# GpSimd multiplies the probabilities of every second attention unit, in place of VectorE

## The chip, the cores and the metric

The kernel runs on one core of one Trainium2 chip. The metric is the device time of one execution in microseconds. The kernel before takes 1446.1 us (median of three runs, 1443.93 to 1446.41). The engines of a core work side by side and are tied together by semaphores only: TensorE (PE in the profile, with PEld for its weight loads), VectorE (DVE), ScalarE (ACT), GpSimd (POOL) and the queue of SyncE (SP).

## The reference, cut to what matters

The program is one inference step of a one-layer decoder: a projection, three kinds of attention or recurrence side by side (forgetting attention, native sparse attention, HGRN2), an output projection, and a mixture of experts. The change lies in the attention over the 1024 prompt tokens. For every head and block of 128 queries four score matrices are formed, softmaxed over the keys and multiplied with values:

```python
def fox_attend(q, qc, qpos, k, v, kc, kpos):          # "fox": all keys up to the query
    s = jnp.einsum('bqhd,bkhd->bhqk', q, k) * scale
    s = s + qc[..., None] - kc[:, :, None, :]           # decay; masked above the diagonal
    p = jax.nn.softmax(s, axis=-1)
    return jnp.einsum('bhqk,bkhd->bqhd', p, v)
# "cmp": masked softmax over up to 63 compressed keys, with a position bias
# "slc": the same over the selected blocks (with 16 blocks and 16 chosen: all keys up to the query)
# "win": the same over the last 512 keys
def masked_softmax(s, valid):
    s = jnp.where(valid, s, NEG)
    m = jnp.max(s, axis=-1, keepdims=True)
    e = jnp.where(valid, jnp.exp(s - m), 0.0)
    return e / jnp.maximum(jnp.sum(e, axis=-1, keepdims=True), TINY)
```

The three sparse results are weighted by gates and added up.

## The kernel before, in words

The prompt attention is the stage `attn` of each engine's program. It runs over 64 units, `PAIRS`: four heads, in each eight blocks of 128 queries (i = 0 to 7), for each block an even unit with the kinds fox and slc and an odd unit with win and cmp. Within a head I number the units u = 0 to 15, so that u = 2i is the even and u = 2i + 1 the odd unit of block i. In an even unit both kinds have 128 (i + 1) keys. In an odd unit win has 128 (i + 1) keys up to 640, and cmp 7, 15, 23 and so on up to 63.

A unit goes through the engines like this (the lines are those of the profile):

- TensorE writes scores into PSUM banks called `vec` (L851). There are four of them, used in turn.
- VectorE reads a bank, adds the bias from SBUF, writes the scores to SBUF and keeps the running minimum; that is one custom instruction with a small read of the accumulator behind it (L1787).
- ScalarE takes the exponentials and their sum (L1360).
- VectorE's `normalise` makes two factors per query from the sums: a `scalar_tensor_tensor` over 2 columns (L1797, event `exps` waited for), a reciprocal over 2 columns (L1799), and then two multiplications of the unit's scores by the factors, in place (L1803, event `probs`).
- TensorE transposes the probabilities, 128 columns at a time, into PSUM banks called `turned` (L863), ScalarE copies them to SBUF (L1353), and TensorE multiplies them with the values (L875, L876 for even units, L882, L884 for odd ones).

Each engine's program is written out in order, and the order is shifted between them. TensorE does scores(d), transposes(d - 2), values(d - 3). VectorE does scores(d), normalise(d - 1). So the probabilities of unit d - 2 are due when TensorE is through with the scores of unit d.

GpSimd has one kind of work in this stage, the table `foxdiag`: the decays of a head with the mask of the diagonal added, 128x1024 (L2167 for head 0, L2170 for the others). The table for head h + 1 needs the decays `cumf` of that head, which VectorE makes behind the scores of u = 8 of head h (`decay_rows`, L1763, eight small instructions), ahead of normalise(7). It is first read at u = 0 of head h + 1.

Of the kernel before, what the change touches and what calls it, by code (L numbers as in the profile page):

```python
# [9 lines left out]
ALU = mybir.AluOpType  # L10
# [3 lines left out]
P = 128  # L14
# [204 lines left out]
def program(nc, ctx, I, O_, known):  # L219
# [26 lines left out]
    def skew(base, offset, *dims):  # L246

        return bass.AP(base.tensor, base.offset + offset, [list(base.ap[0])] + [list(d) for d in dims])
# [55 lines left out]
    small = z.take(4 * 16, 4)  # L304
# [81 lines left out]
    def unit_keys(kind, i):  # L386

        if kind == "cmp":
            return 0, min(8 * i + 7, NCMP), 1
        first = max(0, i - 4) if kind == "win" else 0  # L390
        return first * P, (i + 1 - first) * P, i + 1 - first
# [21 lines left out]
    def score_tiles(d):  # L413

        return Sw[d // 2 % 2] if d % 2 else S[d // 2 % 2]
# [205 lines left out]
    def _(e):  # L621
# [231 lines left out]
        def transposes(d):  # L853
            h, i, kinds = PAIRS[d]
            e.wait_ge(*E.at(("probs", d)))
            for j, kind in enumerate(kinds):
                _, L, nb = unit_keys(kind, i)
                for a in range(0, nb, 4):
                    e.wait_ge(*E.free("turned"))
                    bk = E.bank("turned")  # L860
                    for c in range(min(4, nb - a)):
                        n = min(P, L)
                        last = e.transpose(bk[:n, c * P:(c + 1) * P], score_tiles(d)[j][:, (a + c) * P:(a + c) * P + n], ident)  # L863
                    last.then_inc(*E.filled("turned", ("probs turned", d)))
# [333 lines left out]
    def _(e):  # L1198
# [135 lines left out]
        for it in range(n + 4):  # L1334
            d = it - 4
            if d >= 0 and d % 2:
                h, i, _ = PAIRS[d]
                e.wait_ge(*E.full("summed"))
                bk = E.job("summed")
                e.copy(QT[:, h, i * P:(i + 1) * P], bk[:, 0:P]).then_inc(*E.drained("summed", "prompt attention done"))  # L1340
            d = it - 2
            if 0 <= d < n:
                h, i, kinds = PAIRS[d]
                for j, kind in enumerate(kinds):
                    _, L, nb = unit_keys(kind, i)
                    w = min(P, L)
                    for a in range(0, nb, 4):
                        k = min(4, nb - a)
                        e.wait_ge(*E.full("turned"))
                        bk = E.job("turned")  # L1350
                        if d >= 2:
                            e.wait_ge(*E.at(("values", d - 2)))
                        e.copy(turned_tiles(d)[j][:w, a:a + k, :], bk[:w, 0:k * P].rearrange("p (c n) -> p c n", c=k)).then_inc(*E.drained("turned", ("pt", d, j)))  # L1353
            if it < n:
                h, i, kinds = PAIRS[it]
                for j, kind in enumerate(kinds):
                    _, L, _ = unit_keys(kind, i)
                    e.wait_ge(*E.at(("scores", it, j)))
                    s, sm_ = score_tiles(it)[j][:, 0:L], small[:, it % 4]
                    act(s, s, ACT.Exp, scale=-1.0, bias=sm_[:, least(i, kind, j):least(i, kind, j) + 1], accum_out=sm_[:, j:j + 1]).then_inc(*E.done(("exps", it)))  # L1360
# [127 lines left out]
    def _(e):  # L1488
        E = Engine(ev, e, "vector")
        E.banks = banks  # L1490
        tt, ts, stt, cp = e.tensor_tensor, e.tensor_scalar, e.scalar_tensor_tensor, e.tensor_copy
# [61 lines left out]
        for h in range(H):  # L1553
# [68 lines left out]
            for g in range(2):  # L1622
                e.wait_ge(*E.full("vec"))
                bk = E.job("vec")
                for c in range(4):
                    n = 4 * g + c
                    e.wait_ge(*E.own())
                    i = stt(Sall[:, n + 1, :], Sall[:, n, :], ebl[:, n:n + 1], bk[:, c * P:(c + 1) * P], ALU.mult, ALU.add)
                    i.then_inc(*(E.done() if c < 3 else E.drained("vec", ("states", h))))
            e.wait_ge(*E.at(("s0", h)))  # L1630
            for g in range(2):
# [4 lines left out]
                for c in range(4):  # L1636
                    b = 4 * g + c
                    i = stt(VM[:, b, :], S0[:, b, :], ebl[:, 8 + b:9 + b], bk[:, c * P:(c + 1) * P], ALU.mult, ALU.add)
# [17 lines left out]
        for t in range(NT):  # L1656
# [3 lines left out]
            if t == 8:  # L1660
                for g in range(4):
                    s, o = slice(NS * g, NS * g + NS), slice(g * P, (g + 1) * P)
# [12 lines left out]
        for t in range(NT):  # L1675
# [3 lines left out]
            if t == 8:  # L1679
                for g in range(4):  # L1680
                    s, o = slice(NS * g, NS * g + NS), slice(g * 100, g * 100 + 100)
# [110 lines left out]
        def normalise(d):  # L1792

            h, i, kinds = PAIRS[d]
            sm_ = small[:, d % 4]
            e.wait_ge(*E.at(("exps", d)))
            stt(sm_[:, 2:4], sm_[:, 0:2], TINY, skew(GI, 16 * i + 4 * h + 2 * (d % 2), [1, 2]), ALU.max, ALU.mult).then_inc(*E.done())  # L1797
            e.wait_ge(*E.own())
            e.reciprocal(sm_[:, 2:4], sm_[:, 2:4]).then_inc(*E.done(("factors", d)))  # L1799
            e.wait_ge(*E.own())  # L1800
            for j, kind in enumerate(kinds):
                s = score_tiles(d)[j][:, 0:unit_keys(kind, i)[1]]
                ts(s, s, sm_[:, 2 + j:3 + j], None, ALU.mult).then_inc(*E.done(("probs", d)))  # L1803

        n = len(PAIRS)
        decay_rows(0)
        for it in range(n + 1):
            if it < n:
                scores(it)
                if it % 16 == 8 and it + 16 < n:  # L1810
                    decay_rows(it // 16 + 1)
            if it >= 1:
                normalise(it - 1)
# [310 lines left out]
    def _(e):  # L2124
        E = Engine(ev, e, "gpsimd")
# [37 lines left out]
        for d, (h, i, kinds) in enumerate(PAIRS):  # L2163
            if d % 16 == 0:
                if h == 0:
                    e.wait_ge(*E.at(("cumf", h)))
                    tt(foxdiag[h % 2], cumf[h % 2].rearrange("p (t k) -> p t k", t=8), C["diagmask"].unsqueeze(1).to_broadcast([P, 8, P]), ALU.add).then_inc(*E.done(("foxdiag", h)))  # L2167
            if d % 16 == 9 and h + 1 < H:
                e.wait_ge(*E.at(("cumf", h + 1)))
                tt(foxdiag[(h + 1) % 2], cumf[(h + 1) % 2].rearrange("p (t k) -> p t k", t=8), C["diagmask"].unsqueeze(1).to_broadcast([P, 8, P]), ALU.add).then_inc(*E.done(("foxdiag", h + 1)))  # L2170
        E.stage("p5")
        e.wait_ge(*E.at("prompt attention done"))
        e.wait_ge(*E.at("kv_out"))
# [67 lines left out]
```

## Time and profile before

| quantity | value |
|---|---|
| median of the runs | 1446.1 us |
| the profiled execution's own time | 1446.41 us |
| its span, first to last instruction | 1444.5 us |
| prompt attention in it | about 630 to 868 us |
| PE busy over the span | 1255.2 us, 87% |
| DVE busy | 723.4 us, 50% |
| ACT busy | 419.2 us, 29% |
| POOL busy | 165.4 us, 11% |
| mean granted TensorE clock | 0.933 |

The profiled execution's time is 1.9 us more than its span, and 0.3 us more than the median. The shares are means over very different stages, so that what an edit is worth must be read in the stage that it touches. A busy TensorE in this profile is one whose matmuls follow each other without a hole; the holes are what the stage can win back on the other engines.

### The profile page before, as it was taken

What the parts mean: (1) busy time and instruction counts of PE and PEld (TensorE: products, weight loads), DVE (VectorE), ACT (ScalarE), POOL (GpSimd) and SP (SyncE); (2) the same over time, 40 slices, a digit from 0 to 9 for tenths busy, and PEclk for the clock granted to TensorE, in tenths of its full rate; (3) what the DMA queues carried; (4) which work ended last, traced back from release to release, by engine and by line L of the source; (5) the groups of instructions that cost most, each with busy time, mean ns of one, the idle gap of its engine ahead of it and who ended that gap; (6) DMA issues with size and microseconds to landing.
All of it is one profiled execution on the core that took longest, in us unless ns stands there. A gap on an engine that the chain in (4) does not pass through costs nothing.

```text
span 1444.5 us, 19401 instructions
## 1 busy us (share of the span) xinstructions
PE 1255.2 (87%) x6870; PEld 760.5 (53%) x6870; DVE 723.4 (50%) x1614; ACT 419.2 (29%) x882; POOL 165.4 (11%) x191
## 2 busy tenths in 40 slices
PE   3699999999999999979999999999549999999600
PEld 1468787787877555546676675444223333333200
DVE  5526574675744111257768663345643333333288
ACT  2232231422422010135666762212201111111133
POOL 0003021031211000200000000000011111111130
PEclk9799999999999999959999999999759999999955
DMA  9802020130201204306000006300396967668471
GB/s 307 248 24 59 17 74 1 31 59 17 70 5 46 96 6 83 99 12 168 25 25 1 2 1 190 121 29 30 134 314 219 341 196 269 215 221 282 144 272 69
DMA packets 123237, 163.17 MB, mean 113 GB/s; under 512 B 29763, under 2 KB 98547, under 8 KB 123160
## 3 DMA queue, kind: packets, MB, share of 16 engines
q1 hardware_dynamic: 108840, 112.75, 25.7%
q0 software_dynamic: 14320, 49.41, 9.8%
q8 instruction: 47, 0.77, 0.2%
q14 instruction: 30, 0.25, 0.1%
HBM read 225.01 MB, written 36.45 MB: 181 GB/s over the span
## 4 chain that ended last, share of the span: by engine, by line
PE 78%; DVE 14%; ACT 3%; DMA 2%; issue 2%; SPq 0%; POOL 0%; DVEq 0%; ACTq 0%; POOLq 0%
PE act L650 15%; PE vec L1157 11%; PE vec L917 9%; PE vec L679 7%; PE vec L851 5%; PE vec L700 4%; PE act L863 4%; PE act L875 2%; PE act L1170 2%; PE vec L1170 2%; PE act L882 2%; DVE arena L2116 2%; PE vec L815 1%; DMA arena<-x_rows,arena 1%; PE vec L660 1%
## 5 line engine op out<-in xcount | busy, mean ns | idle before, releaser
L650 PE MATMUL act<-arena 128*128 128x352 f32 x768 | 239.1, 467 | 0.4 <-issue 0.4
L650 PEld LDWEIGHTS act<-arena 128*128 128x128 f32 x768 | 145.5, 193 | 76.9 <-issue 3.4
L1157 PE MATMUL vec<-arena 128*64 128x512 f32 x768 | 172.5, 601 | 2.9 <-issue 2.9
L917 PE MATMUL vec<-arena 128*128 128x512 f32 (+1 forms) x288 | 126.3, 593 | 0.4 <-ACT arena L1340 0.4
L1787 DVE CUSTOM_DVE_ANT_0 arena<-vec,arena 128x128 f32<-128x128 f32 (+9 forms) x200 | 86.8, 459 | 60.3 <-PE vec L851 50.3
L1157 PEld LDWEIGHTS vec<-arena 128*64 128x64 f32 x768 | 54.1, 138 | 104.4 <-issue 104.1
L679 PE MATMUL vec<-arena 128*128 128x512 f32 (+1 forms) x256 | 99.9, 546 | 0.0
L2079 DVE TENSOR_SCALAR arena<-arena 128x256 f32<-128x256 f32 x24 | 7.1, 296 | 172.1 <-ACT arena L1451 172.1
L1353 ACT COPY arena<-act 128x512 f32<-128x512 f32 (+11 forms) x176 | 63.7, 431 | 81.7 <-PE act L863 81.6
L851 PE MATMUL vec<-arena 64*128 64x512 f32 (+11 forms) x352 | 84.2, 475 | 3.2 <-DVE arena L1787 2.0
L917 PEld LDWEIGHTS vec<-arena 128*128 128x128 f32 (+1 forms) x288 | 50.8, 180 | 67.5 <-issue 66.2
L1360 ACT ACTIVATE arena<-arena 128x640 f32<-128x640 f32 (+15 forms) x128 | 81.6, 643 | 16.5 <-DVE arena L1787 16.4
L863 PE MATMUL act<-arena 128*128 128x128 f32 (+4 forms) x440 | 66.3, 288 | 6.8 <-DVE arena L1803 6.1
L679 PEld LDWEIGHTS vec<-arena 128*128 128x128 f32 x256 | 47.8, 190 | 44.9 <-issue 27.7
L1613 DVE COPY_PREDICATED arena<-arena,vec 128x512 f32<-128x512 int32 x64 | 44.5, 729 | 48.3 <-PE vec L700 46.5
L700 PEld LDWEIGHTS vec<-arena 128*128 128x128 f32 x512 | 61.9, 192 | 9.3 <-DVE arena L1596 3.2
L660 PE MATMUL vec<-arena 128*128 128x128 f32 (+1 forms) x576 | 65.3, 275 | 0.0
L660 PEld LDWEIGHTS vec<-arena 128*128 128x128 f32 (+1 forms) x576 | 64.5, 183 | 1.3
L700 PE MATMUL vec<-arena 128*128 128x128 f32 x512 | 62.7, 276 | 2.4 <-DVE arena L1596 2.4
L863 PEld LDWEIGHTS act<-arena 128*128 128x128 f32 (+4 forms) x440 | 47.3, 143 | 28.0 <-DVE arena L1803 11.5
L851 PEld LDWEIGHTS vec<-arena 64*128 64x128 f32 x352 | 42.3, 195 | 34.2 <-issue 14.9
L1451 ACT ACTIVATE arena<-vec 128x256 f32<-128x256 f32 x24 | 9.2, 385 | 165.7 <-PE vec L1157 165.7
(371 smaller groups left out, 1832.8 us busy)
## 6 DMA issues: line engine op xcount, KB each, us to landing
arena<-in_exp_w SPq DMA_DIRECT2D x144, 1024.0 KB
y_rows<-arena POOLq DMA_DIRECT2D x48, 256.0 KB, 5.1
arena<-in_w_in SPq DMA_DIRECT2D x16, 512.0 KB, 6.8
arena<-in_x_prompt SPq DMA_DIRECT2D x8, 512.0 KB, 10.0
x_spill<-arena POOLq DMA_DIRECT2D x8, 512.0 KB, 5.6
arena<-x_spill SPq DMA_DIRECT2D x8, 512.0 KB, 4.9
arena<-in_cache_fox_kv SPq DMA_DIRECT2D x16, 256.0 KB, 3.5
x_rows<-arena POOLq DMA_DIRECT2D x8, 512.0 KB, 2.9
```

What stands on the lines that cost most here:

```text
L650: last = mm(bk[:, 0:n], W[k % 2][:, c, m * P:(m + 1) * P], xT[:, c, a:a + n], start=c == 0, stop=c == NC - 1)
L660: last = mm(bk[:r, o:o + P], xT[:, c, t * P:t * P + r], W[h % 2][:, c, 3 * P:4 * P], start=c == 0, stop=c == NC - 1)
L679: last = mm(bk[:r, 0:width], xT[:, c, t * P:t * P + r], w[:, c, 0:width], start=c == 0, stop=c == NC - 1)
L700: last = mm(bk[:, c * P:(c + 1) * P], a[:, ch], b[:, ch], start=True, stop=True)
L851: mm(bk[:, 0:n], QT[s, h, i * P:(i + 1) * P], k[:, first + a:first + a + n], start=True, stop=True).then_inc(*E.filled("vec"))
L863: last = e.transpose(bk[:n, c * P:(c + 1) * P], score_tiles(d)[j][:, (a + c) * P:(a + c) * P + n], ident)
L917: last = mm(bk[:r], src, Wo[:, c, half * 512:(half + 1) * 512], start=c == 0, stop=c == NC - 1)
L1157: last = mm(gu_bank[p][o], xgT[p][:, c, o], Wgu[:, slot, c, :], start=c == 0, stop=c == NC - 1)
L1170: last = mm(dn_bank[half][o], hT[p][:, f, o], Wd[:, slot, f, half * 512:(half + 1) * 512], start=f == 0, stop=f == 1)
L1353: e.copy(turned_tiles(d)[j][:w, a:a + k, :], bk[:w, 0:k * P].rearrange("p (c n) -> p c n", c=k)).then_inc(*E.drained("turned", ("pt", d, j)))
L1360: act(s, s, ACT.Exp, scale=-1.0, bias=sm_[:, least(i, kind, j):least(i, kind, j) + 1], accum_out=sm_[:, j:j + 1]).then_inc(*E.done(("exps" ...
L1787: ins = e.tensor_tensor_reduce(out=s[:, a + o:a + o + w], in0=bk[:, o:o + w], in1=bias, scale=1.0, scalar=prior, op0=ALU.add, op1=ALU.min, ...
```

## The change

VectorE keeps the first two steps of `normalise` (L1797, L1799) for all units, and the two multiplications of the even units. The two multiplications of an odd unit are issued by GpSimd, which first waits for the event `factors` of that unit (the reciprocal). TensorE's wait for `probs` of an odd unit is thereby a wait for GpSimd's counter. In GpSimd's order they stand behind the `foxdiag` of the same iteration.

```diff
             e.reciprocal(sm_[:, 2:4], sm_[:, 2:4]).then_inc(*E.done(("factors", d)))
-            e.wait_ge(*E.own())
-            for j, kind in enumerate(kinds):
-                s = score_tiles(d)[j][:, 0:unit_keys(kind, i)[1]]
-                ts(s, s, sm_[:, 2 + j:3 + j], None, ALU.mult).then_inc(*E.done(("probs", d)))
+            if d % 2 == 0:
+                e.wait_ge(*E.own())
+                L = (i + 1) * P
+                for j in range(2):
+                    s = score_tiles(d)[j][:, 0:L]
+                    ts(s, s, sm_[:, 2 + j:3 + j], None, ALU.mult).then_inc(*E.done(("probs", d)))
...
         # in GpSimd's loop over the units, behind foxdiag:
+            if d % 2:
+                e.wait_ge(*E.at(("factors", d)))
+                for j, kind in enumerate(kinds):
+                    s = score_tiles(d)[j][:, 0:unit_keys(kind, i)[1]]
+                    e.tensor_scalar(s, s, small[:, d % 4, 2 + j:3 + j], None, ALU.mult).then_inc(*E.done(("probs", d)))
```

64 of VectorE's 128 multiplications move. The orders of TensorE and ScalarE stay as they are. VectorE's order at the decays of the next head, which lie between the scores of u = 8 and normalise(7); L1763 is the last step of the decays, ISA 128x512 the custom instruction on the scores of u = 9. Before:

```order
L1763 TENSOR_SCALAR arena<-vec,arena 128x128 x7
L1797 SCALAR_TENSOR_TENSOR arena<-arena 128x2
L1799 RECIPROCAL arena<-arena 128x2
L1803 TENSOR_SCALAR arena<-arena 128x512
L1803 TENSOR_SCALAR arena<-arena 128x31
L1787 ISA arena<-vec,arena 128x512
L1787 ISA arena 128x1
L1787 ISA arena<-vec,arena 128x39
L1787 ISA arena 128x1
L1787 ISA arena<-vec,arena 128x128
L1787 ISA arena 128x1
L1797 SCALAR_TENSOR_TENSOR arena<-arena 128x2
```

VectorE's order at the same place after the change (L1805 is what L1803 was, for u = 8 here):

```order
L1763 TENSOR_SCALAR arena<-vec,arena 128x128 x7
L1797 SCALAR_TENSOR_TENSOR arena<-arena 128x2
L1799 RECIPROCAL arena<-arena 128x2
L1787 ISA arena<-vec,arena 128x512
L1787 ISA arena 128x1
L1787 ISA arena<-vec,arena 128x39
L1787 ISA arena 128x1
L1787 ISA arena<-vec,arena 128x128
L1787 ISA arena 128x1
L1797 SCALAR_TENSOR_TENSOR arena<-arena 128x2
L1799 RECIPROCAL arena<-arena 128x2
L1805 TENSOR_SCALAR arena<-arena 128x640 x2
```

The 512 and the 31 columns of u = 7 have left VectorE's queue, and the scores of u = 9 stand right behind the reciprocal. GpSimd's order before, for the whole attention (L2176 belongs to the stage behind it):

```order
L2167 TENSOR_TENSOR arena<-arena 128x1024
L2170 TENSOR_TENSOR arena<-arena 128x1024 x3
L2176 MEMSET arena 128x512
L2176 MEMSET arena 128x256 x2
L2176 MEMSET arena 128x128
```

GpSimd's order after the change, from u = 5 to u = 9 of a head (L2172 is the `foxdiag` of the next head, L2177 the multiplications):

```order
L2177 TENSOR_SCALAR arena<-arena 128x384
L2177 TENSOR_SCALAR arena<-arena 128x23
L2177 TENSOR_SCALAR arena<-arena 128x512
L2177 TENSOR_SCALAR arena<-arena 128x31
L2172 TENSOR_TENSOR arena<-arena 128x1024
L2177 TENSOR_SCALAR arena<-arena 128x640
L2177 TENSOR_SCALAR arena<-arena 128x39
```

The `foxdiag` of the next head, which had an empty queue ahead of it, now stands behind the multiplications of u = 7, which wait for the reciprocal that VectorE issues behind the decays.

## Rows read from the trace of the kernel before

**Rows 1.** Busy us by engine in two stretches: stretch, length, engines, PEclk, DMA, GB/s
```profile
728.00:752.00 24.00, 23.98 (x200) 17.52 (x199) 16.60 (x63) 17.04 (x48) 0.00 (x0) 1.00 0.11 37
716.00:720.00 4.00, 2.24 (x12) 1.39 (x11) 3.86 (x11) 1.38 (x5) 2.00 (x1) 1.00 0.00 0
```
**Rows 2.** Waits from 630 to 862 us: engine, line, waited for, total us, times, longest
```profile
DVE arena L1787 <- PE vec L851: 50.3, 55, 2.4
PE act L863 <- DVE arena L1803: 6.1, 5, 1.8
```
**Rows 3.** GpSimd's tables: one in the timeline, and the group of three
```profile
716.86 2.00 POOL L2170 TENSOR_TENSOR arena<-arena 128x1024 f32<-128x1024 f32 x1 [57.89 <-DVE arena L1797]
...
L2170 POOL TENSOR_TENSOR arena<-arena 128x1024 f32<-128x1024 f32 x3 | 6.0, 1999 | 141.0 <-DVE arena L1797 141.0
```
**Rows 4.** VectorE's timeline in head 1, at the next decays: start us, us, instruction
```profile
716.69 0.15 DVE L1797 SCALAR_TENSOR_TENSOR arena<-arena 128x2 f32<-128x2 f32 x1
716.88 0.17 DVE L1799 RECIPROCAL arena<-arena 128x2 f32<-128x2 f32 x1
717.08 2.21 DVE L1803 TENSOR_SCALAR arena<-arena 128x512 f32<-128x512 f32 x2
...
720.45 0.15 DVE L1797 SCALAR_TENSOR_TENSOR arena<-arena 128x2 f32<-128x2 f32 x1
...
720.84 1.02 DVE L1803 TENSOR_SCALAR arena<-arena 128x640 f32<-128x640 f32 x2
```
**Rows 5.** TensorE's timeline at the same place
```profile
716.02 1.57 PE L851 MATMUL vec<-arena 64*128 64x512 f32 x6
719.35 0.77 PE L863 MATMUL act<-arena 128*128 128x128 f32 x5 [1.76 <-DVE arena L1803]
...
722.57 1.66 PE L863 MATMUL act<-arena 128*128 128x128 f32 x10
```
**Rows 6.** GpSimd: a line's min/median/max ns; groups with busy us, mean ns, idle before
```profile
L2142 POOL TENSOR_TENSOR arena<-arena x28: 1097/1292/1555, 113.8 to 422.3; 128x512 f32<-128x512 f32 x20, 128x528 f32<-128x528 f32 x8
...
L2134 POOL TENSOR_TENSOR arena<-arena 128x1056 f32<-128x1056 f32 x4 | 11.2, 2795 | 125.6 <-DVE arena L1576 125.6
...
L2176 POOL MEMSET arena<- 128x256 f32 x2 | 0.6, 312 | 0.0
...
L2176 POOL MEMSET arena<- 128x512 f32 x1 | 0.5, 525 | 90.8 <-ACT arena L1340 90.8
```
**Rows 7.** Timelines of both engines at the odd units 3, 5 and 9 of head 1
```profile
702.92 0.50 DVE L1803 TENSOR_SCALAR arena<-arena 128x256 f32<-128x256 f32 x2
...
707.73 0.57 DVE L1803 TENSOR_SCALAR arena<-arena 128x384 f32<-128x384 f32 x2
...
725.56 0.71 DVE L1803 TENSOR_SCALAR arena<-arena 128x640 f32<-128x640 f32 x2
...
703.48 0.55 PE L863 MATMUL act<-arena 128*128 128x128 f32 x3
...
708.55 0.66 PE L863 MATMUL act<-arena 128*128 128x128 f32 x4
...
727.04 0.33 PE L863 MATMUL act<-arena 128*128 128x128 f32 x1
```
**Rows 8.** Both engines in an earlier stage; of two lines min/median/max ns
```profile
108.24 2.79 POOL L2134 TENSOR_TENSOR arena<-arena 128x1056 f32<-128x1056 f32 x1 [52.20 <-DVE arena L1576]
...
L1592 DVE TENSOR_TENSOR arena<-arena x28: 684/704/2925, 108.7 to 420.4; 128x512 f32<-128x512 f32 x20, 128x528 f32<-128x528 f32 x8
...
L1602 DVE TENSOR_TENSOR arena<-vec,arena x8: 675/677/691, 116.4 to 392.1; 128x512 f32<-128x512 f32 x8
```
**Rows 9.** Head 0: TensorE at the same place, and a stretch with the clock
```profile
659.46 0.86 PE L863 MATMUL act<-arena 128*128 128x128 f32 x5 [1.76 <-DVE arena L1803]
...
668.72 0.55 PE L863 MATMUL act<-arena 128*128 128x128 f32 x3
...
662.00:663.00 1.00, 1.00 (x6) 0.51 (x4) 0.00 (x0) 0.02 (x1) 0.00 (x0) 0.50 0.09 17
```

## The prediction

> **What bounds the kernel now.** I first read the busy times by stretch. In the wide units of the attention TensorE is busy 23.98 of 24 us at the full granted clock, VectorE 16.60 [rows 1]. Then the waits: VectorE waits for TensorE's scores 50.3 us in 55 places, TensorE for VectorE's multiplications 6.1 us in five, the longest 1.8 [rows 2]. So VectorE isn't the bound, and work taken from it is worth nothing by itself. Time lies only in TensorE's holes. One is plain: from 716 to 720 us TensorE is busy for 2.24 of 4 us [rows 1], and the timelines say why. VectorE's multiplications of unit 7 start at 717.08 and last 2.21 us; TensorE's transposes of that unit stand at 719.35 behind a hole of 1.76 [rows 4, 5]. A `foxdiag` runs on GpSimd from 716.86 to 718.86 [rows 3], and it holds the multiplication up: the pair of 384 and 23 columns takes 0.57 us, that of 640 and 39 takes 0.71 [rows 7], so this one of 512 and 31 should take some 0.64. The group of such tables has three members [rows 3], one in each of heads 0 to 2, and the hole in head 0 is also 1.76 [rows 9].
>
> **What the change removes there.** VectorE issues no multiplication of unit 7. GpSimd does it first and the table behind it. I work out head 1, by the profiled times.
>
> What one pair costs on GpSimd no row shows. The nearest are: a memset, which only writes, at 312 ns for 256 and 525 ns for 512 columns [rows 6], hence 0.83 ns a column and 0.1 us fixed, the low end; a two-input operation, 2.00 us for 1024 columns [rows 3] and at least 1.10 for 512 [rows 6], hence 1.76 ns a column and 0.2 fixed; and 2.79 us for 1056 columns under load [rows 6, 8], 2.65 a column, the high end. A multiplication by a factor reads one array and writes one; I take 1.0 ns a column and 0.15 us fixed, nearest to the memset. GpSimd's start behind VectorE's result I take at 0.08 us, a little over the 0.06 that TensorE needs (719.35 against an end at 719.29 [rows 4, 5]).
>
> - The reciprocal ends at 717.05 [rows 4]. GpSimd starts at 717.13 and needs 0.66 + 0.18 = 0.84, so 717.97. The transposes start 0.06 us behind at 718.03 instead of 719.35: 1.32 us gained.
> - What is late next: the table now runs from 717.97 to 719.97. VectorE meanwhile does the scores of unit 9 and comes to the factors of unit 8, two SBUF inputs, and to its multiplications, both of the kinds that have been seen waiting for GpSimd [rows 4, 8]. From that factor step to the multiplications are 0.39 us, and these take 1.02 [rows 4], so they end at 719.97 + 1.41 = 721.38, and the transposes of unit 8 start at 721.44. TensorE's own work would bring it there at 718.03 + 3.22 = 721.25 [rows 5]. Against 722.57 the gain is 1.13.
> - Head 2 is like head 1; in head 0 the transposes of unit 8 come later (half clock, below), so its 1.32 stays.
>
> That makes 1.32 + 2 x 1.13 = 3.58 us.
>
> In head 0 the granted clock is 0.5 (1.2 GHz) in the stretch behind the hole [rows 9], and from the transposes of unit 7 to those of unit 9 it takes 668.72 - 659.46 = 9.26 us, in head 1 727.04 - 719.35 = 7.69 at full clock [rows 5, 7, 9]. Those 1.57 us lie behind a hole of 1.76, which would shrink to 0.4; but the same hole in head 1 cost no clock [rows 1]. I count half, 0.8 us.
>
> **What it adds.** TensorE waits for GpSimd in every odd unit. VectorE's pair started 0.03 us behind the reciprocal and took 0.50 us (unit 3), 0.57 (unit 5) and 0.71 (unit 9); TensorE took up the result 0.06, 0.25 and 0.77 us behind its end [rows 7], so that 0, 0.19 and 0.71 us are free.
>
> - Unit 3, 256 + 15 columns: 0.08 + 0.41 + 0.17 = 0.65 against 0.53, late by 0.12, nothing free. Three heads (head 0 has half clock and room there): 0.36 us.
> - Unit 5, 384 + 23: 0.08 + 0.53 + 0.17 = 0.79 against 0.60, 0.19 late and 0.19 free: 0.
> - Unit 9, 640 + 39: 0.08 + 0.79 + 0.19 = 1.06 against 0.74, 0.32 late, 0.71 free: 0. Later units have the same 640 columns and more of TensorE's work ahead, and unit 1 is the narrowest; I count none of them.
>
> Behind the waiting GpSimd instruction only the next odd unit and the tables are queued, and a table isn't read until the next head. VectorE's freed time lies in its waits for scores [rows 2]: 0. The even multiplications meet GpSimd only beside the tables: a side unit's GpSimd pair is through in about 1 us, while VectorE first has two or three score instructions of the next unit.
>
> Sum: -3.58 - 0.8 + 0.36 = -4.0 us on 1446.41, that is 1442.4; the median lies 0.3 below the profiled time, and I say 1442.3.
>
> **What the skill says.** The rows show a VectorE operation with two SBUF inputs at 2.9 instead of 0.68 us beside a GpSimd operation, and one with a PSUM and an SBUF input at 675 to 691 ns whatever ran beside it [rows 8]. The Trainium skill (SBUF — State Buffer, "Who interferes with whom") has this as a lock on a shared port pair, taken for a whole instruction by GpSimd and by VectorE's two-port modes or two-input operations; the trace agrees. By that rule the score instructions stay free, as in my sum. The skill's Perfetto Trace Analysis ("Optimizing Scalar/DVE Operations") warns that moving work between these two engines might not help for that reason; taken literally it would make the gain zero. GPSIMD Engine Reference ("4.1 Engine selection") calls one-input operations about line rate there; an estimate of 0.83 ns a column at its 1.2 GHz would take 0.5 us off my loss and add as much gain.
>
> **The rivals.**
>
> *GpSimd multiplies at the two-input rate* (1.76 ns a column, 0.2 fixed). Unit 3: 0.08 + 0.65 + 0.23 = 0.96 against 0.53, 0.43 late, three times 1.3. Unit 5: 1.20 against 0.60, less the free 0.19, three times 0.41: 1.2. Unit 7 of head 3 about 0.4, unit 9 1.68 against 0.74 less 0.71, with head 3 some 1.2 together. Loss 4.1. At the tables GpSimd ends at 718.49, the gain is 0.8 at unit 7, and the table then ends at 720.49 and unit 8's pair at 721.90: 0.6. Gain 2.0 and no clock won. 1448. For it: the only elementwise operations in the trace run so. Against: they read two arrays.
>
> *The custom score instruction is held too.* Its inputs are like those of the free one in [rows 8], but it never ran beside GpSimd in the trace. Then VectorE stands through unit 7's pair and the table until 719.97, has 2.65 us to the end of unit 8's pair (719.21 to 721.86 now), so 722.62: nothing gained in heads 1 and 2. -1.3 + 0.4 = -0.9: 1445.3.
>
> *Slower: GpSimd is slow enough to be the bound of odd units.* Place: TensorE's transposes of units 3 to 13. At 2.65 ns a column unit 9 takes 2.31 us against 0.74, 0.86 beyond what is free, unit 3 0.67, unit 5 0.77; over 18 such units with 0.5 to 0.9 each about 13 us, less 0.6 at the tables: 1459. Interpolated between this and the two-input rate, it is slower than before by 0.2% from about 1.85 ns a column. Against: those 2.79 us include a wait, since VectorE's operation of 0.68 us had started before and the next took until GpSimd was through [rows 8].
>
> **How the numbers follow.** The forecast has 0.63, the two-input rate 0.14, the held score instruction 0.11, the slow GpSimd 0.12. About 0.2% (2.9 us) is what a measurement can tell from no change. The forecast's own range is 1440.5 (the whole clock term, the memset's rate) to 1444.5 (no clock, losses doubled); three quarters of it lie below 1443.2, which gives faster 0.47. The two-input rate and the held instruction count as same, with the rest of the forecast: 0.39, and the slower one, with a little of the two-input case, 0.14. The range for 8 in 10 is 1440 to 1448.5.
>
> **What the profile would show.** GpSimd's pair of 640 and 39 columns in about 1 us; the hole ahead of unit 7's transposes 0.4 instead of 1.76 us, in three heads; the table right behind unit 7's pair, and unit 8's factor step or multiplication lengthened beside it; score instructions as long as before, also beside GpSimd's work; no new waits of TensorE for GpSimd above 0.2 us. I am wrong if GpSimd's 640 columns take over 1.2 us, or if TensorE's holes at unit 8 take back what unit 7 gives.

## The result and the profile after

| | before | after |
|---|---|---|
| median, us (four runs each, on one chip) | 1445.01 | 1465.81 |
| lowest to highest | 1443.4 to 1446.41 | 1460.02 to 1466.76 |
| profiled execution's own time / its span | 1446.41 / 1444.5 | 1462.62 / 1460.7 |

The ratio is 1.0128, 95% interval 1.01 to 1.0155; it takes in three more runs of the kernel after (1462.62, 1462.97 and 1459.45), so it is a little below the quotient of the two medians. The change makes the kernel 1.3% slower. I had forecast 4 us less; it is about 20 us more. The page of the kernel after, its busy line and the shares of the chain that ended last:

```profile
PE 1260.3 (86%) x6870; PEld 762.0 (52%) x6870; DVE 704.1 (48%) x1550; ACT 419.4 (29%) x882; POOL 225.9 (15%) x255
...
PE 72%; DVE 17%; POOL 4%; ACT 3%; DMA 2%; issue 2%; SPq 0%; DVEq 0%; ACTq 0%; POOLq 0%
```

GpSimd has 60.5 us more to do, VectorE 19.3 less: each microsecond taken from VectorE costs three on GpSimd. And GpSimd, which was 0% of that chain before, is now 4% of it. The groups of GpSimd's multiplications, shapes apart (busy us, mean ns of one, idle before them and what ended it); the neighbours from which I guessed them are in [rows 3, 6]:

```profile
L2177 POOL TENSOR_SCALAR arena<-arena 128x640 f32<-128x640 f32 x16 | 30.2, 1886 | 95.8 <-DVE arena L1799 95.8
L2172 POOL TENSOR_TENSOR arena<-arena 128x1024 f32<-128x1024 f32 x3 | 6.9, 2310 | 0.0
...
L2177 POOL TENSOR_SCALAR arena<-arena 128x256 f32<-128x256 f32 x4 | 3.7, 927 | 15.8 <-DVE arena L1799 15.8
```

640 columns take 1886 ns, 256 take 927: 2.50 ns a column, and 0.29 us fixed. That is 2.5 times the rate I took, and nearly the far end of my range (2.65). VectorE needed 0.71 us for a pair of 640 and 39 columns [rows 7]; GpSimd needs 1.89 + 0.40. The waits in the attention, which answer to [rows 2]:

```profile
DVE arena L1787 <- PE vec L851: 88.3, 61, 3.2
...
PE act L863 <- POOL arena L2177: 18.8, 25, 1.6
```

TensorE's wait for multiplications grew from 6.1 us in five places to 18.8 in 25, none of them long. VectorE's freed time became waiting for scores, 50.3 before and 88.3 now, in a stage that is also 18 us longer. Now head 1 in GpSimd's timeline, at units 3, 5, 7 and 9, and the decays' table behind unit 7:

```profile
696.78 1.25 POOL L2177 TENSOR_SCALAR arena<-arena 128x256 f32<-128x256 f32 x2 [3.67 <-DVE arena L1799]
...
703.54 1.58 POOL L2177 TENSOR_SCALAR arena<-arena 128x384 f32<-128x384 f32 x2 [5.51 <-DVE arena L1799]
...
713.76 1.92 POOL L2177 TENSOR_SCALAR arena<-arena 128x512 f32<-128x512 f32 x2 [8.64 <-DVE arena L1799]
715.64 2.33 POOL L2172 TENSOR_TENSOR arena<-arena 128x1024 f32<-128x1024 f32 x1
...
723.55 2.26 POOL L2177 TENSOR_SCALAR arena<-arena 128x640 f32<-128x640 f32 x2 [5.58 <-DVE arena L1799]
```

and TensorE's transposes of the same units 3, 5, 7, 8 and 9; before, the holes ahead of them were 0 at units 3, 5 and 9 [rows 7] and 1.76 at unit 7 [rows 5]:

```profile
698.08 0.55 PE L863 MATMUL act<-arena 128*128 128x128 f32 x3 [0.85 <-POOL arena L2177]
...
705.18 0.44 PE L863 MATMUL act<-arena 128*128 128x128 f32 x2 [0.37 <-POOL arena L2177]
...
715.74 1.17 PE L863 MATMUL act<-arena 128*128 128x128 f32 x5 [1.53 <-POOL arena L2177]
...
720.53 1.66 PE L863 MATMUL act<-arena 128*128 128x128 f32 x10
725.87 1.28 PE L863 MATMUL act<-arena 128*128 128x128 f32 x6 [0.80 <-POOL arena L2177]
```

The hole at unit 7, on which the whole gain rested, went from 1.76 to 1.53. The slow multiplication took the place of the held one. Every odd unit from 3 to 13, but for unit 7, has a new hole, in all four heads (unit 7 of head 3, which had none, has one of 0.94). VectorE's timeline around 715 us shows that what I said of the table came true otherwise:

```profile
713.50 0.17 DVE L1799 RECIPROCAL arena<-arena 128x2 f32<-128x2 f32 x1
...
713.91 0.69 DVE L1787 CUSTOM_DVE_ANT_0 arena<-vec,arena 128x512 f32<-128x512 f32 x1 [0.24 <-PE vec L851]
...
715.17 0.16 DVE L1797 SCALAR_TENSOR_TENSOR arena<-arena 128x2 f32<-128x2 f32 x1
...
715.56 2.76 DVE L1805 TENSOR_SCALAR arena<-arena 128x640 f32<-128x640 f32 x2
```

GpSimd starts 0.09 us behind the reciprocal's end. The score instruction takes 0.69 us beside GpSimd's work, no longer than alone. The pair of unit 8 beside the table takes 2.76 us instead of 1.02 [rows 4]. TensorE doesn't wait for it: it has enough of its own.

The holes aren't all. Two readings of the granted clock in head 1, stretches behind the holes of units 7 and 9 (length; busy us of PE, PEld, DVE, ACT, POOL; clock; DMA share; GB/s):

```profile
716.00:719.40 3.40, 3.40 (x23) 2.54 (x23) 2.32 (x2) 1.87 (x6) 1.97 (x1) 0.51 0.01 2
726.20:729.60 3.40, 3.40 (x28) 2.70 (x27) 1.32 (x3) 2.04 (x7) 0.00 (x0) 0.50 0.02 5
```

TensorE is busy in every microsecond of them, at its lower level of 1.2 GHz. To see how much the two things cost, the windows of heads 1, 2 and 3, each from one head's last output copy to the next one's; first of before:

```profile
698.84:757.16 58.32, 55.66 (x435) 39.01 (x436) 42.66 (x172) 37.62 (x117) 2.00 (x1) 1.00 0.05 16
757.16:815.47 58.31, 55.66 (x435) 39.00 (x436) 42.62 (x172) 37.59 (x117) 2.00 (x1) 1.00 0.01 2
815.47:867.66 52.19, 51.60 (x404) 35.77 (x404) 35.10 (x142) 34.80 (x102) 0.00 (x0) 1.00 0.00 1
```

and of after:

```profile
692.64:758.71 66.07, 60.63 (x435) 42.05 (x436) 37.88 (x156) 37.67 (x117) 17.13 (x18) 0.92 0.04 14
758.71:823.74 65.03, 59.10 (x435) 41.14 (x435) 37.86 (x156) 37.63 (x116) 17.05 (x18) 0.95 0.01 2
823.74:881.80 58.06, 53.44 (x404) 36.66 (x404) 30.63 (x128) 34.77 (x103) 14.41 (x16) 0.97 0.00 1
```

The three heads take 20.34 us longer. Length less PE's busy time is the holes: 5.90 us before, 15.99 after, 10.1 more. The other 10.2 us are PE's busy time itself, 162.92 before and 173.17 after, for the same matmuls: about 20 us at 1.2 GHz, in six stretches of 3.4 us, each 1.7 us longer than at 2.4 GHz. So half of the loss is holes, and half is clock in stretches that stand behind holes; that the holes cause it is taken up below. Over the whole attention the profiled executions differ by 18.2 us (260.0 against 241.8), since head 0 came out 2 us shorter; the stage before it was 4.1 us shorter and the rest 2.1 longer, neither of which holds anything of the change.

### The profile page after: what moved, and what is told of

The parts are those of the page before. It is cut to its first block, busy times and chain, and to the rows that moved or that the text cites. A ratio compares the mean times of both kernels' runs of the same rounds, so it can differ in the third digit from the quotient of the medians.

```text
span 1460.7 us, 19401 instructions
## 1 busy us (share of the span) xinstructions
PE 1260.3 (86%) x6870; PEld 762.0 (52%) x6870; DVE 704.1 (48%) x1550; ACT 419.4 (29%) x882; POOL 225.9 (15%) x255
## 4 chain that ended last, share of the span: by engine, by line
PE 72%; DVE 17%; POOL 4%; ACT 3%; DMA 2%; issue 2%; SPq 0%; DVEq 0%; ACTq 0%; POOLq 0%
PE act L650 15%; PE vec L1157 11%; PE vec L917 9%; PE vec L679 7%; PE vec L700 4%; POOL arena L2177 3%; DVE arena L1787 3%; PE act L875 3%; PE vec L851 3%; PE act L863 3%; PE act L1170 2%; PE vec L1170 2%; DVE arena L2118 2%; PE vec L815 1%; DMA arena<-x_rows,arena 1%
## 5 line engine op out<-in xcount | busy, mean ns | idle before, releaser
L1787 DVE CUSTOM_DVE_ANT_0 arena<-vec,arena 128x128 f32<-128x128 f32 (+9 forms) x200 | 86.8, 458 | 98.2 <-PE vec L851 88.3
L2177 POOL TENSOR_SCALAR arena<-arena 128x640 f32<-128x640 f32 (+4 forms) x64 | 59.4, 940 | 185.1 <-DVE arena L1799 185.1
L863 PE MATMUL act<-arena 128*128 128x128 f32 (+4 forms) x440 | 67.4, 291 | 19.8 <-POOL arena L2177 18.8
L2200 POOL DMA_DIRECT2D y_rows<-arena x48 | 25.7, 540 | 239.3 <-DVE arena L2093 238.8
```

Of the source, the lines that this page charges most:

```text
L1787: ins = e.tensor_tensor_reduce(out=s[:, a + o:a + o + w], in0=bk[:, o:o + w], in1=bias, scale=1.0, scalar=prior, op0=ALU.add, op1=ALU.min, ...
L2177: e.tensor_scalar(s, s, small[:, d % 4, 2 + j:3 + j], None, ALU.mult).then_inc(*E.done(("probs", d)))
```

## The experiments

Nine more kernels ran, and two were run a second time. All edits stand against the changed kernel unless I say otherwise. Ratios are against the kernel before on the same chip, with 95% intervals.

### Is it the instruction? The same columns by a two-input multiplication

```diff
-    e.tensor_scalar(s, s, small[:, d % 4, 2 + j:3 + j], None, ALU.mult)
+    tt(s, s, small[:, d % 4, 2 + j:3 + j].to_broadcast([P, unit_keys(kind, i)[1]]), ALU.mult)
```

> The changed kernel, but GpSimd multiplies the odd units' scores by the factor in the two-input form (tensor_tensor with the factor repeated along the row) in place of tensor_scalar. Nothing else differs: same hand-offs, same order, same shared memory. Theory A (the change costs what GpSimd's slow multiplication adds to the path from the factors to the transposes, 1.89 us for 640 columns): the two-input form has run at 1.10 us for 512 and 2.00 for 1024 columns, so 640 columns should take about 1.33; TensorE's waits for GpSimd, 18.8 us in 25 places, shrink to about 6, the half-clock stretches behind them become fewer, and the time falls from 1465 to about 1450. Rival B (the hand-off between engines, or GpSimd's presence on the shared memory port, is what costs): two inputs load the port more, so the time stays at 1460 to 1470 or grows.

Measured: 1441.21 us, ratio 0.9973 (0.9962 to 0.9983), 9 us better than I expected. GpSimd's groups, and TensorE's waits for them:

```profile
L2177 POOL TENSOR_TENSOR arena<-arena 128x640 f32<-128x640 f32 x16 | 20.1, 1253 | 95.3 <-DVE arena L1799 95.3
...
L2177 POOL TENSOR_TENSOR arena<-arena 128x256 f32<-128x256 f32 x4 | 2.5, 614 | 17.0 <-DVE arena L1799 17.0
```

```profile
PE act L863 <- POOL arena L2177: 4.7, 11, 0.9
```

It has two inputs to read, the scores and the repeated factor, and is faster: 1.67 ns a column and 0.19 us fixed. With nothing else changed, the median is 24.6 us below that of the change, and a little below before. This is the run that settles the cause: the order, the queues and the added wait are those of the change; only the price differs. Head 1 with it:

```profile
694.02:752.10 58.08, 55.80 (x435) 39.01 (x436) 37.66 (x156) 37.65 (x117) 11.46 (x18) 1.00 0.05 16
```

The hole at unit 7 shrank to 0.8 us, and holes of 0.4 and 0.2 came at units 3 and 5, so the head is only 0.24 us shorter than before; head 3, which has no table to gain from, is 0.95 longer. The rest of the 4 us lies in head 0 and ahead of the attention, where two executions of one kernel differ by as much (below). The runs show that the median is lower than before; they don't show by what.

### Which form costs what

Only unit 15 of each head is left to GpSimd, each time in another form. Heads 0 and 1 leave the true factor out.

```diff
+    if h == 0:   ins = e.tensor_scalar(s, s, 0.01, None, ALU.mult)
+    elif h == 1: ins = e.tensor_copy(s, s)
+    elif h == 2: ins = tt(s, s, f.to_broadcast([P, n]), ALU.mult)
+    else:        ins = e.tensor_scalar(s, s, f, None, ALU.mult)      # only in unit 15 of each head
```

> As the kernel in which GpSimd has only unit 15 of each head, but in another form in each head, in place over 640 and 63 columns: head 0 a multiplication by a constant (0.01, in place of the factor), head 1 a copy (the factor left out), head 2 the two-input multiplication by the repeated factor, head 3 the multiplication by the pointer to the factor as in the change. So the probabilities of unit 15 are not normalised in heads 0 and 1. It measures the disputed price by itself: head 3 1.89 us and head 2 1.25 us for 640 columns as seen. If the pointer operand is what costs, the constant takes about 0.7 to 0.8 us; if the program that GpSimd runs for this operation is what costs, the constant takes 1.9 too. The copy should take about 0.65 us, by one column for each 0.83 ns. The time stays that of before.

```profile
L2184 POOL TENSOR_SCALAR arena<-arena 128x640 f32<-128x640 f32 x1 | 1.9, 1884 | 51.6 <-DVE arena L1799 51.6
L2178 POOL TENSOR_SCALAR arena<-arena 128x640 f32<-128x640 f32 x1 | 1.8, 1827 | 32.8 <-DVE arena L1799 32.8
L2182 POOL TENSOR_TENSOR arena<-arena 128x640 f32<-128x640 f32 x1 | 1.3, 1255 | 31.5 <-DVE arena L1799 31.5
L2180 POOL COPY arena<-arena 128x640 f32<-128x640 f32 x1 | 0.7, 715 | 31.3 <-DVE arena L1799 31.3
```

One execution took 1441.9 us, the kernel before beside it 1444.09. For 640 columns: 1884 ns with a factor per row, 1827 with a constant, 1255 by two inputs, 715 for a copy. So neither the factor's address nor the memory traffic makes the instruction dear: a copy reads and writes the same bytes in 0.72 us. It is this operation on this engine.

### Only where there is room: unit 15 alone

```diff
-            if d % 2:
+            if d % 2 and i == 7:          # VectorE does the others
```

> The changed kernel with GpSimd's multiplications kept for unit 15 of each head alone (block 7); VectorE does the odd units of blocks 0 to 6 as before the change. In the trace of before, TensorE took up the result of unit 15 some 2.3 us after it was ready, and GpSimd's pair ends about 1.7 us later than VectorE's. Theory A: it fits in, no wait of TensorE for GpSimd in these four places, and the time is that of before within 0.2% (1445). Rival B (a hand-off to GpSimd costs by itself, or its port use slows VectorE): four of 32 units moved, so an eighth of the 18 us, slower by about 2 us.

1444.06 us, ratio 0.9989 (0.9977 to 1.0001), as expected. Its head 1, against 58.32 before:

```profile
698.15:756.47 58.32, 55.66 (x435) 39.02 (x436) 41.89 (x170) 37.61 (x117) 4.32 (x3) 1.00 0.05 16
```

PE's columns are those of before to 0.01 us. GpSimd's 2.3 us in unit 15 are hidden even at the slow price, and VectorE's relief there brings nothing: both as the prediction had them. Unit 15 alone is so well off: even units 11 and 13, as wide and nearly as late, have holes of 0.5 us after the change.

### Waiting out GpSimd: one unit more between scores and transposes

```diff
-            if 2 <= d < n + 2: transposes(d - 2)
-            if d >= 3: values(d - 3)
+            if 3 <= d < n + 3: transposes(d - 3)
+            if d >= 4: values(d - 4)          # ScalarE's copies shifted alike
```

> The changed kernel, all odd units still multiplied by GpSimd in the slow form, but TensorE transposes a unit one unit later (scores(d), transposes(d - 3), values(d - 4) in place of d - 2 and d - 3) and ScalarE copies in the same order. Each multiplication thereby has one more unit of TensorE's work, some 2 to 4 us, before it is due. Theory A (the loss is only that the multiplication is late for the transposes): the 25 waits of TensorE for GpSimd (18.8 us) go to nearly nothing and the half-clock stretches inside the attention with them; one head takes about 57 us (58.3 before the change, 65 to 66 after it), and the time comes to 1433 to 1440 with 2 us more at the stage's end. Rival B (port or hand-off): GpSimd's and VectorE's operations lie beside each other more than now, VectorE's even multiplications get longer, and the time stays over 1450.

1440.1 us, ratio 0.9967 (0.9954 to 0.9981). TensorE has no wait for GpSimd left, at GpSimd's slow price. Heads 1 and 2:

```profile
695.87:752.22 56.35, 55.50 (x436) 39.02 (x437) 36.25 (x156) 37.76 (x117) 18.82 (x17) 1.00 0.05 16
752.22:808.56 56.34, 55.48 (x436) 39.01 (x436) 36.26 (x156) 37.79 (x116) 18.82 (x17) 1.00 0.01 2
```

1.96 us less than before a head, and no half clock: with the holes gone, the clock loss is gone too. Some of what this order gives is lost at the start of the attention, where TensorE is at half clock from 626 to 654 us in this profile (before: 629 to 646).

### The gain without the cost: the table alone moved

Against the kernel before, on GpSimd:

```diff
                 e.wait_ge(*E.at(("cumf", h + 1)))
+                e.wait_ge(*E.at(("probs", d)))
                 tt(foxdiag[(h + 1) % 2], ...)
```

> The kernel before, all multiplications on VectorE, with one more wait on GpSimd: the table foxdiag of the next head starts only when the probabilities of unit 9 are done, which leaves about 2.2 us until VectorE's next two-port operation. It tests what I took for the gain of the change. Theory A: the multiplication of unit 7 takes 0.49 us instead of 2.06, the three holes of 1.76 us ahead of the transposes of unit 7 go, perhaps a half-clock stretch in head 0 with them: faster by 4.5 to 6.5 us, 1439 to 1441. Rival: the hole moves to another multiplication beside the table, or TensorE waits for the decays there anyway: within 1 us of before.

1434.82 us, ratio 0.9937 (0.9917 to 0.9957), 4 us better than the expectation's edge. VectorE's pair of unit 7 in its timeline (2.21 us before, [rows 4]), the transposes behind it in TensorE's (a hole of 1.76 before, [rows 5]), and the window of head 1:

```profile
706.31 0.64 DVE L1803 TENSOR_SCALAR arena<-arena 128x512 f32<-128x512 f32 x2
```

```profile
707.01 0.77 PE L863 MATMUL act<-arena 128*128 128x128 f32 x5 [0.18 <-DVE arena L1803]
```

```profile
688.08:744.82 56.74, 55.66 (x435) 39.01 (x435) 41.23 (x172) 37.60 (x116) 2.00 (x1) 1.00 0.05 16
```

Head 1 is 1.58 us shorter than before, all of it hole. So the part of the prediction on what makes the hole of unit 7 was right, the pair's 0.64 us to the hundredth, and it can be had with one wait and no work moved. Three heads give 4.7 us. The median fell by 10.5. To see where the rest is, both kernels ran once more, unchanged.

> The kernel before, unchanged, for a second profile of head 0. In the first the granted clock was 0.5 from 629 to 646 us, at the start of the attention, and from 660 to 663. If this belongs to the kernel, it is there again and the attention takes 241 to 242 us; if it is chance, head 0 is shorter by up to 6 us, as with the table moved. Heads 1 and 2 take 58.3 us each either way.

> The kernel with the table made to wait for unit 9, unchanged, for a second profile of head 0. In the first its attention took 231.9 us, with half clock up to 634.7 us and none after. If the shorter head 0 belongs to the edit, it is there again; if it is chance, it may be up to 6 us longer. Heads 1 and 2 take 56.7 us each either way.

1444.61 and 1437.97 us, one execution each. Head 1, head 2 and a stretch of head 2 in this second profile of before:

```profile
690.54:750.48 59.94, 57.28 (x435) 39.68 (x435) 42.63 (x172) 37.55 (x116) 2.00 (x1) 0.97 0.05 15
750.48:811.67 61.19, 58.54 (x435) 40.68 (x436) 42.60 (x172) 37.55 (x117) 2.00 (x1) 0.94 0.01 2
...
771.00:777.00 6.00, 6.00 (x29) 3.62 (x29) 2.88 (x11) 1.87 (x6) 0.00 (x0) 0.50 0.01 3
```

The holes are those of the first profile (2.66 and 2.65 us a head), and yet PE's busy time is 1.6 and 2.9 us more, at half clock behind the same hole at unit 7. So a hole of 1.76 us sometimes costs clock and sometimes doesn't.

The 58.3 us that I expected for these heads either way didn't come; that the stage as a whole took 242 us, as expected, is luck, since head 0 was 4.1 us shorter by chance. Counting heads 1 and 2 of the four profiles that have it (before twice, unit 15 alone, the forms), half clock follows in four of eight: in both heads of two profiles, in neither of the other two. PE's busy time is 0.94 us more on average over the eight. In the twelve such heads of the six profiles in which the hole is gone (the table moved, twice, and four others) it follows in none.

The attention stage took 241.8 and 242.2 us in the two profiles of before, 231.9 and 235.5 with the table moved. Of the 10.5 us at the median, 4.7 are holes; the clock behind three such holes would be 2.8 by the average above, and some 3 us are left over.

### Only the narrow half on GpSimd

VectorE multiplies `win`, GpSimd `cmp` (at most 63 columns), with an event of its own that TensorE waits for ahead of the `cmp` transposes. Against the kernel before:

```diff
+                if kind == "cmp":
+                    e.wait_ge(*E.at(("cmp probs", d)))
...
-            for j, kind in enumerate(kinds):
+            for j, kind in enumerate(kinds[:2 - d % 2]):      # VectorE
...
+            if d % 2:
+                e.wait_ge(*E.at(("factors", d)))
+                s = score_tiles(d)[1][:, 0:unit_keys("cmp", i)[1]]   # GpSimd
+                e.tensor_scalar(s, s, small[:, d % 4, 3:4], None, ALU.mult).then_inc(*E.done(("cmp probs", d)))
```

> The kernel before with GpSimd doing only the narrow cmp multiplication (7 to 63 columns, 0.33 to 0.46 us on GpSimd) of every odd unit, beside VectorE's win multiplication (0.29 to 0.56 us). All 32 hand-offs of the change are there, the slow wide multiplication isn't. Theory A: GpSimd is through before or with VectorE, so that no odd unit is late by more than 0.1 us; and since the table of the next head now stands behind the cmp part of unit 7, VectorE's win part of unit 7 gets ahead of it, and three holes of 1.76 us shrink: 1440 to 1444. Rival B (hand-off or port): at least half of the 18 us stays, 1453 or more.

1431.93 us, ratio 0.991 (0.9895 to 0.9924): the lowest median of all, 8 us below the range that I expected. The window of its head 1, and the timelines of VectorE and of GpSimd at unit 7:

```profile
686.50:743.21 56.71, 55.65 (x435) 39.00 (x435) 40.62 (x164) 37.68 (x116) 7.27 (x9) 1.00 0.05 16
```

```profile
704.62 0.49 DVE L1805 TENSOR_SCALAR arena<-arena 128x512 f32<-128x512 f32 x1
```

```profile
704.68 0.67 POOL L2176 TENSOR_SCALAR arena<-arena 128x31 f32<-128x31 f32 x1 [8.76 <-DVE arena L1801]
705.31 2.00 POOL L2172 TENSOR_TENSOR arena<-arena 128x1024 f32<-128x1024 f32 x1
```

The small multiplication keeps the table behind VectorE's wide one, as the added wait does in the version before: 1.61 us less a head, against 1.58. Do the two add up? Here the table waits for `probs` as well and stands behind GpSimd's multiplication:

> The kernel in which GpSimd multiplies only the cmp part of the odd units (1431.9 us), with the table foxdiag moved behind unit 9's cmp part and made to wait for unit 9's win part on VectorE. Theory A: what is left of TensorE's waits for VectorE at the tables (1.8 us in 5 places) shrinks to that at the end of the stage: 1430 to 1432, at most 1.5 us better. Rival: the gains of the two edits add up in full (13 and 10 us), near 1422.

1434.49 us, ratio 0.992 (0.9903 to 0.9937), 2.5 us above the range that I expected. Heads 1 and 2 are 0.23 us shorter still (56.48 and 56.49), which the median doesn't show; the rival, that the two gains add up to 1422, fell. Nor does one unit more of distance help:

> The last kernel with TensorE's transposes one unit later as well. Theory A: hardly any hole is left in the attention that a later due time could fill (heads 1 and 2 are TensorE's own work), and the pipeline is one unit longer at its end, so 1430 to 1434, the same within 0.2% of the kernel without the lag. Rival: the matmuls still wait in ways that the busy time hides, and it gains 3 us or more.

1439.58 us, ratio 0.9962 (0.9948 to 0.9977), 5 us slower than without it, with heads 1 and 2 as short as 56.35. I had expected 1430 to 1434. The loss is at the attention's start again: the two profiles with this distance have 41 us at half clock from 608 us on, the eleven others 20 to 38. These traces don't show why.

### The table ahead of unit 7

```diff
-            if d % 16 == 9 and h + 1 < H:
+            if d % 16 == 7 and h + 1 < H:
```

> The changed kernel with the table foxdiag of the next head put back where it ran before, ahead of the multiplication of unit 7 in GpSimd's order. Theory A: GpSimd's order matters where its work is due; the table (2.0 us) now delays unit 7's pair, so the three holes ahead of unit 7's transposes grow from 1.5 to about 3.3 us, while unit 8's pair on VectorE no longer meets the table: slower than the changed kernel by 3 to 7 us, 1468 to 1472. Rival (the place of the table is worth nothing, as the hole at unit 7 is as long as the slow pair makes it anyway): within 2 us of the changed kernel.

1474.23 us, ratio 1.0205 (1.0187 to 1.0222). GpSimd at unit 7 of head 1, and TensorE behind it:

```profile
719.58 2.00 POOL L2172 TENSOR_TENSOR arena<-arena 128x1024 f32<-128x1024 f32 x1 [8.36 <-DVE arena L1797]
721.55 2.15 POOL L2177 TENSOR_SCALAR arena<-arena 128x512 f32<-128x512 f32 x2
```

```profile
723.76 0.83 PE L863 MATMUL act<-arena 128*128 128x128 f32 x5 [3.45 <-POOL arena L2177]
```

The hole grows by 1.92 us, about the table's length. So the order that the change chose on GpSimd is the better one of the two. Three such places cost 8.4 us at the median (2 us above the range that I expected): 5.8 are holes, and the rest, which I put down to the clock, isn't shown apart.

## Why the prediction was wrong

- **What bounds the kernel: right.** TensorE's holes, VectorE's relief worth nothing, the hole at unit 7 made by the table. The moved table gives 1.58 us a head with nothing else changed.
- **GpSimd's price: wrong, and the step that failed.** I took 1.0 ns a column and 0.15 us fixed, "nearest to the memset", and measured were 2.50 and 0.29, so that 640 columns took 1.89 us, beyond the 1.2 that I had named as the sign of being wrong. The argument was that the instruction reads one array and writes one. The forms show that such counting doesn't rank GpSimd's operations: two inputs are faster than one. I had bounds of 0.83 and 2.65, both from rows, with the truth between them. What was wrong was to put 0.63 of the chance at the low end, on a likeness, when the only rows with arithmetic in them ran at 1.76 and more.
- **What it adds: 0.36 us forecast.** With the measured price the steps that I used give the right holes. Unit 3: 0.09 + 1.25 = 1.34 against 0.53, so 0.81 late; measured 0.85. Unit 9: 0.09 + 2.26 = 2.35 against 0.74, less 0.71 free, so 0.90; measured 0.80. Unit 5: 1.67 against 0.60 less 0.19, so 0.88; measured 0.80 in heads 0 and 2, and 0.37 in head 1, where a stretch of half clock from 698.9 us on makes the transposes late anyway. Units 11 and 13, which I left out of the count, have 0.5 each. All in all there are 10.1 us more of holes in heads 1 to 3. The slow rival, which I gave 0.12, had the place and nearly the size: "about 13 us" of new holes in four heads, and 14.2 measured.
- **The gain at the tables: 3.58 us forecast, 0.6 in holes measured** (the hole of unit 7 is 1.53, 1.53 and 1.59 us in heads 0 to 2, against 1.76). It hung on the same price: 1.92 us for the pair instead of 0.84.
- **The clock: sized on one side only.** I counted 0.8 us won by a smaller hole in head 0, and in no case anything lost by new ones. It is 10.2 us, half of what the change costs in heads 1 to 3, and why the slow rival's 1459 was still short of 1465.8. That the hole of head 1 had cost no clock in one profile was an outcome of one execution; the second profile of before has the same hole with the cost. The runs without holes had no half clock in these heads, also with all of GpSimd's work kept (one unit more of distance), so I take the holes as its cause. That is argued and not shown: these runs still have 0.9 to 1.1 us of holes a head, and the two-input version, with 2.3 us in holes of up to 0.9, had no half clock in heads 1 to 3 either. Which hole is followed by one isn't settled.
- **The two-input rival: right in its rate** (1.76 and 0.2 taken, 1.67 and 0.19 measured), too high in its time: 1448 against 1441.2. In heads 1 to 3 of its profile this version costs 0.5 us in all; the rest of the difference is in head 0 and outside the stage.
- **The held score instruction: fell.** 512 columns take 692 ns beside GpSimd's work and 689 alone.
- **Two slips in the sums:** 0.3 below 1442.4 is 1442.1, and I said 1442.3. And the estimate at 0.83 ns a column can't take 0.5 us off a loss of 0.36. Neither bears on the outcome. Measured, the copy of 640 columns comes to 1.1 ns a column with its fixed part; the multiplication is at 2.50 without it.
- **The port:** work moved from VectorE to GpSimd didn't help here, as the Trainium skill warns (Perfetto Trace Analysis, "Optimizing Scalar/DVE Operations"), but not for the reason given there, the shared port: in the changed kernel no VectorE instruction is longer by more than 3 ns beside GpSimd's multiplications by a factor. What is held there, the pair of unit 8, is held by the table, and TensorE doesn't wait for it. In another order such multiplications do lengthen VectorE's (below).
- **Open:** how long TensorE stays at half clock at the start of the attention. It is 20 to 41 us from 608 us on in the thirteen profiles, in patterns that differ between two executions of one kernel, and it moves the medians by some microseconds. The 4 us of the two-input version, and 3 of the 10.5 of the moved table, lie in such differences and are only argued.

## What to carry to other kernels

Before moving an operation to GpSimd, measure that very operation there at its width. Its neighbours in the trace don't give the price, and the form with two inputs can be the faster one. Work moved off an engine that isn't the bound brings nothing; what it can do is lengthen the chain between two engines in each iteration, so compare its new length with what is free there, at the worst end of the price. Price a new hole ahead of TensorE with the clock behind it, 0.6 us a hole on average after the change and 1 us behind those of 1.76 us before, and look at two profiles before calling a hole free of it. And where one GpSimd operation holds up a VectorE one, try first to start it a little later: one wait gave 1.58 us a head here, and 10 at the median, 3 of them unexplained.

## What the runs showed of the hardware

- GpSimd, f32, SBUF to SBUF, 128 rows: multiplication by a factor per row 2.50 ns a column and 0.29 us, the same in the two-input form with the factor repeated 1.67 and 0.19, a copy of 640 columns 0.715 us.
- The two engines don't meet alike in all GpSimd operations. The two-input one holds up VectorE's steps that have their inputs in SBUF. With the two-input version, VectorE's small two-input step, 0.15 us alone, beside the table:

```profile
714.09 2.00 POOL L2172 TENSOR_TENSOR arena<-arena 128x1024 f32<-128x1024 f32 x1
...
714.33 1.78 DVE L1797 SCALAR_TENSOR_TENSOR arena<-arena 128x2 f32<-128x2 f32 x1
```

- GpSimd's multiplication by a factor doesn't hold these small steps: in the version with one unit more of distance, 22 of them lie wholly beside it, at 156 ns (153 to 160). There it is GpSimd's pair that grows, beside VectorE's wide pair. First GpSimd's timeline, a pair beside VectorE's and one alone, then VectorE's:

```profile
718.18 2.93 POOL L2177 TENSOR_SCALAR arena<-arena 128x640 f32<-128x640 f32 x2 [1.92 <-DVE arena L1799]
...
734.98 2.30 POOL L2177 TENSOR_SCALAR arena<-arena 128x640 f32<-128x640 f32 x2 [6.13 <-DVE arena L1799]
```

```profile
719.81 1.22 DVE L1805 TENSOR_SCALAR arena<-arena 128x768 f32<-128x768 f32 x2
```

- VectorE's wide multiplications can grow too. In the version with the table first they start inside GpSimd's pair of unit 7 (721.55 to 723.70 us, shown there), and the pair of 640 columns takes 1.64 instead of 1.02 us, its two parts 0.76 and 0.96 instead of 0.55 each. The first one ends 0.5 us before GpSimd's multiplication of 512 columns does, so it isn't held to that one's end. In the version with one unit more of distance 384 columns take 0.46 instead of 0.42 us inside such a multiplication. The pair in the version with the table first:

```profile
721.83 1.64 DVE L1805 TENSOR_SCALAR arena<-arena 128x640 f32<-128x640 f32 x2
```

The Trainium skill (SBUF — State Buffer, "Who interferes with whom") has it that the engine which takes the shared port pair first keeps it for its whole instruction, and that the other is blocked fully. The trace agrees for GpSimd's two-input operation. It doesn't for the multiplication by a factor: beside it the small VectorE steps run at their own speed, and the wide ones of the version with the table first are lengthened by 0.2 and 0.4 us where full blocking would have cost the first one 1.3 us.
